# Products with low parts last in each dot and sum, and an earlier split of U on ScalarE

## The reference

```python
def one(tb):                                        # a block of tokens
    ...                                             # scores, two top-k: experts e, gates g
    a = jax.nn.gelu(jnp.einsum('td,thkd->thk', tb, u_tab[e]), approximate=False)
    return jnp.einsum('thk,thkd->td', (g * a).astype(tb.dtype), v_tab[e])
```

## Time and profile before

| | us |
|---|---|
| median of 3 runs (4121.81 to 4129.34) | 4121.95 |
| the profiled execution, its own time | 4132.75 |
| its span from first to last instruction | 4130.9 |
| experts, from the first dot (2104.42) to the last add | about 1941 |
| TensorE busy in the span | 3358.8 (81%) |
| VectorE busy in the span | 2775.2 (67%) |
| GpSimd busy in the span | 1710.3 (41%) |
| ScalarE busy in the span | 1352.9 (33%) |

### The profile page before, as it was taken

One profiled execution on the slowest core, in us unless ns is written; L12 is line 12 of the kernel. 1 busy time (PEld: TensorE's weight loads), 2 busy tenths in 40 slices (PEclk: granted clock), 3 DMA queues, 4 the chain that ended last, 5 costly groups with the idle time before them and its releaser, 6 DMA issues. The chain is left out here.

```text
span 4130.9 us, 59356 instructions
## 1 busy us (share of the span) xinstructions
PE 3358.8 (81%) x20729; PEld 2933.1 (71%) x20729; DVE 2775.2 (67%) x5874; ACT 1352.9 (33%) x3186; POOL 1710.3 (41%) x1341
## 2 busy tenths in 40 slices
PE   6799678565776886466669999999999999999995
PEld 3577455211466786355569999999999999999994
DVE  3114586200024059999968999889899989998885
ACT  3000366100022111578723333333333333333331
POOL 1001000000030432678855556556655655655550
PEclk8899899778678998667779999999999999999997
DMA  6766544799522332254578898889888888988984
GB/s 232 256 223 221 166 151 134 304 408 415 213 87 74 96 107 81 62 117 111 123 257 314 315 332 324 310 315 327 316 309 324 320 320 319 328 318 302 330 286 154
DMA packets 389553, 1001.91 MB, mean 243 GB/s; under 512 B 187044, under 2 KB 232975, under 8 KB 325688
## 3 DMA queue, kind: packets, MB, share of 16 engines
q1 hardware_dynamic: 323768, 491.18, 35.0%
q0 software_dynamic: 62656, 469.86, 31.5%
q10 hardware_dynamic: 2944, 38.77, 2.6%
HBM read 914.75 MB, written 152.04 MB: 258 GB/s over the span
## 5 line engine op out<-in xcount | busy, mean ns | idle before, releaser
L2163 DVE CUSTOM_DVE_ANT_0 e_uv<-e_uv,e_h 128x1024 f32<-128x1024 f32 x416 | 717.2, 1724 | 86.4 <-DMA e_uv<-peer_uv,k_g_idx 85.2
L2232 POOL DMA_INDIRECT e_uv<-peer_uv,k_g_idx x416 | 520.2, 1251 | 547.4 <-DVE e_pY L2175 503.1
L1470 PE MATMUL e_po<-e_ph,e_vh 128*128 128x320 f32 x2048 | 646.8, 316 | 55.9 <-DVE k_OT L2207 49.5
L1470 PE MATMUL e_pa<-k_hi_d,e_uh 128*128 128x320 f32 x2048 | 640.4, 313 | 59.7 <-POOL e_ul L2223 43.3
L1472 PE MATMUL e_pa<-k_hi_d,e_ul 128*128 128x320 f32 x2048 | 634.4, 310 | 0.0
L1471 PE MATMUL e_pa<-k_lo_d,e_uh 128*128 128x320 f32 x2048 | 634.3, 310 | 0.0
L1472 PE MATMUL e_po<-e_ph,e_vl 128*128 128x320 f32 x2048 | 634.0, 310 | 0.0
L1471 PE MATMUL e_po<-e_pl,e_vh 128*128 128x320 f32 x2048 | 634.0, 310 | 0.0
L2175 DVE SCALAR_TENSOR_TENSOR e_pY<-e_uv,e_wts,e_pY 128x1024 f32<-128x1024 f32 x412 | 525.8, 1276 | 0.0
L1470 PEld LDWEIGHTS e_po<-e_ph,e_vh 128*128 128x128 f32 x2048 | 385.5, 188 | 79.0 <-DVE k_OT L2207 64.9
L1470 PEld LDWEIGHTS e_pa<-k_hi_d,e_uh 128*128 128x128 f32 x2048 | 385.9, 188 | 73.0 <-issue 51.8
(11 more groups left out here) (301 smaller groups left out, 5974.9 us busy)
## 6 DMA issues: line engine op xcount, KB each, us to landing
s_kv<-kv_pages SPq DMA_DIRECT2D x128, 512.0 KB, 6.8
s_kv<-kv_state SPq DMA_DIRECT2D x32, 2048.0 KB, 17.3
e_v<-peer_uv SPq DMA_DIRECT2D x128, 512.0 KB, 6.4
e_u<-peer_ut SPq DMA_DIRECT2D x126, 512.0 KB, 6.1
s_g<-r_G SPq DMA_DIRECT2D x10, 4096.0 KB, 21.1
k_OT<-s_g SPq DMA_DIRECT2D x128, 320.0 KB, 5.7
k_win_sample<-state_k_win ACTq DMA_DIRECT2D x28, 1168.0 KB
v_win_sample<-state_v_win POOLq DMA_DIRECT2D x28, 1168.0 KB, 9.8
```

Source lines behind the costliest of these rows:

```text
L1470: nc.tensor.matmul(out, lhs_hi, rhs_hi, start=start, stop=False)
L2163: nc.vector.tensor_tensor_reduce(uv[:, r, 0:D], uv[:, r, 0:D], h[:], 1.0, 0.0, ALU.mult, ALU.add, dots[:, r:r + 1]).then_inc(row_dotted, 1)
L2232: nc.gpsimd.indirect_dma_start(uv[:, s % RING], None, io["peer_uv"], bass.IndirectOffsetOnAxis(ap=keep.g_idx[:, s:s + 1], axis=0),).then_i ...
```

## The change

In `dot`, TensorE waits for the high part of U alone, makes the 16 products with it (high x high and high x low for 8 k), then in the first block waits for the low part, and makes the 8 products with it. In `out`, each sum is now four products vh x ph, four vl x ph and four vh x pl; ahead of them it waits for `vh_done` and `ph_done`, ahead of the second four (n = 0 only) for `vl_done`, ahead of the third four (k = 0 only) for `pl_done`. On ScalarE, U's splits of m = 1 and m = 3 go from behind e_ph to ahead of the wait for `p_done`, between the gelu and e_ph.

```diff
 def dot(i, c):
-    pe.wait_ge(ul_done, CQ * i + c + 1)
+    pe.wait_ge(uh_done, CQ * i + c + 1)
     for b in range(NBD):
         m = NBD * c + b
         pe.wait_ge(p_done, DOTS * i + m + 1)
         cols = slice(b * WD, (b + 1) * WD)
         for k in range(KC):
-            x = split_product(nc, pa[:, m % 2, 0:WD], uh[:, c % 2, k], ul[:, c % 2, k],
-                              keep.hi_d[:, k, cols], keep.lo_d[:, k, cols], k == 0, k == KC - 1)
+            nc.tensor.matmul(pa[:, m % 2, 0:WD], uh[:, c % 2, k], keep.hi_d[:, k, cols], start=(k == 0), stop=False)
+            nc.tensor.matmul(pa[:, m % 2, 0:WD], uh[:, c % 2, k], keep.lo_d[:, k, cols], start=False, stop=False)
+
+        if b == 0:
+            pe.wait_ge(ul_done, CQ * i + c + 1)
+        for k in range(KC):
+            x = nc.tensor.matmul(pa[:, m % 2, 0:WD], ul[:, c % 2, k], keep.hi_d[:, k, cols], start=False,
+                                 stop=(k == KC - 1))
         x.then_inc(dotted, 1)

 def out(i):
-    pe.wait_ge(vl_done, CQ * i + CQ)
+    pe.wait_ge(vh_done, CQ * i + CQ)
     for b in range(NBD):
         cols = slice(b * WD, (b + 1) * WD)
-        pe.wait_ge(pl_done, DOTS * i + NBD * (CQ - 2) + b + 1)
+        pe.wait_ge(ph_done, DOTS * i + NBD * (CQ - 2) + b + 1)
         for k in range(KC):
             n = KC * b + k
+            rows = slice(k * P, (k + 1) * P)
             pe.wait_ge(added, OUTS * i + n + 1)
             for c in range(CQ):
                 if k == 0 and c == CQ - 1:
-                    pe.wait_ge(pl_done, DOTS * i + NBD * (CQ - 1) + b + 1)
-                x = split_product(nc, po[:, n % SUMS, 0:WD], vh[:, c, k * P:(k + 1) * P],
-                                  vl[:, c, k * P:(k + 1) * P], ph[:, c, cols], pl[:, c, cols],
-                                  c == 0, c == CQ - 1)
+                    pe.wait_ge(ph_done, DOTS * i + NBD * (CQ - 1) + b + 1)
+                nc.tensor.matmul(po[:, n % SUMS, 0:WD], vh[:, c, rows], ph[:, c, cols], start=(c == 0), stop=False)
+
+            if n == 0:
+                pe.wait_ge(vl_done, CQ * i + CQ)
+            for c in range(CQ):
+                nc.tensor.matmul(po[:, n % SUMS, 0:WD], vl[:, c, rows], ph[:, c, cols], start=False, stop=False)
+            if k == 0:
+                pe.wait_ge(pl_done, DOTS * i + NBD * (CQ - 1) + b + 1)
+            for c in range(CQ):
+                x = nc.tensor.matmul(po[:, n % SUMS, 0:WD], vh[:, c, rows], pl[:, c, cols], start=False,
+                                     stop=(c == CQ - 1))
             x.then_inc(summed, 1)
...
 def gelus(i, m):
     ...
     nc.scalar.activation(pa[:, m % 2, 0:WD], pa[:, m % 2, 0:WD], ACT.Gelu).then_inc(gelu_done, 1)
+    if b == 1 and c < 2:
+        split_u(CQ * i + 2 + c)
     act.wait_ge(p_done, n + 3)
...
         gelus(i, m)
-        if m % NBD == 1 and m // NBD < 2:
-            split_u(CQ * i + 2 + m // NBD)
         if m in V_AT:
```

## The result

The changed kernel takes 4168.4 us in the median of 4 runs (4163.97 to 4176.4), the kernel before 4123.51 us (4 runs): the ratio is 1.0108, 95% interval 1.0087 to 1.013. It is slower, by 45 us (36 to 54). Its profiled execution took 4164.41 us, 31.7 us more than that of before (4132.75), its span is 4162.6 us. Measured again later beside other kernels, the pair gave 1.0093 (1.0067 to 1.012).

The account below looks back on a forecast made before the run. The bound was taken to be the circle VectorE, ScalarE, VectorE, with GpSimd entering through VectorE. Parts 0, 0 and 30 x 1.1 = +33 us gave 4166 us profiled, 4155 us median; own range 4140 to 4170, 8-in-10 range 4118 to 4172.

Parts of the forecast that it names:

- Part 1: TensorE's new order and waits: the stall before m=4 goes, but ScalarE hardly waits for TensorE; 0, bounds -22.7 and 0.
- Rival (a): TensorE's stalls were the bound, so removing 22.7 us of them gives 4099 us; chance 6%.
- Part 2: U's split at m=1 moved up on ScalarE: GpSimd is held by its own queue, e_ul starts no earlier; 0.
- Part 3: U's split at m=3 moved up: e_ul asks for the ports 1.06 us earlier, ahead of e_pl; +1.1 us a round.
- the replay: The round shown, recomputed from e_ul of m=3 to e_act of m=6: sum 2.20 us late, +1.1 us at the end.
- the collision: At m=3, e_ul comes in while the row dot runs and goes ahead of e_pl; next sum starts 2.20 us late.
- Rival (b): At m=3 VectorE's queue keeps the ports and e_pl goes first, or the meeting is missed; 4122 us, chance 15%.
- the precedent of the earlier trace: First round of the kernel before: e_ul, arriving inside a row dot, went ahead of e_pl, which took 2.67 us.
- Rival (c): The collision at m=3 happens but nothing comes back: 2.20 x 31 = +68 us, 4190 us; chance 7%.
- The price of a round: Delay of e_act of m=6 per round, +1.1 us, range 0.6 to 1.6, counted for 30 rounds.
- the sentence that nothing in the sums gives time back: After e_act of m=6, VectorE is full in the sums and TensorE waits for it, so the +1.1 us stays.

Follow-up runs that it names:

- the held one: Changed kernel plus a GpSimd wait for e_pl of m=3 before it subtracts U's chunk there, against the kernel before: 4121.44 us, 1.0016.
- the kernel with all subtractions placed: TensorE's new order, ScalarE's U splits as before, U's and V's subtractions on GpSimd moved by waits and order, against the kernel before: 4037.05 us, 0.9799.
- the kernel with the early load: Changed kernel with SyncE issuing U's load for m=3 ahead of V's, about 2 us earlier, against the kernel before: 4169.75 us, 1.0137.

## Why the prediction was right, point by point

The sign, the half of the change that does it, and the place were right, and the time lies in the range and in the narrower one (4140 to 4170); 4155 was 13 us short. For the profiled execution the sum gave 4166 us, and it took 4164.41. The 13 us lie in the step from there to the median: the profiled execution of before was 10.8 us above its median, which the prediction took off, and the one of the changed kernel was 4.0 us below its own. So how close 4155 came owes something to luck.

*Part 1, TensorE's order, 0:* shown by that half alone (1.0006). Standing for 0 was the row that the gelu waits 8.4 us for TensorE. The stall went, and a new one before dot m=6, forecast at 1.7 us, came: 1.72 us in the median round. Rival (a) fell with this. The prediction counts three new waits a sum; they are three in all 16 sums of a round, which changes nothing in its sum.

*Part 2, the split at m=1, 0:* shown by the kernel with it alone (1.0003).

*Part 3, the split at m=3:* the replay held step by step. In us behind the start of e_vl of m=2, forecast and traced in the round shown above: e_ul 3.64 and 3.81, sum 6.83 and 6.85, e_act of m=4 8.02 and 8.05, its row dot 8.42 and 8.45, e_act of m=6 13.27 and 13.20. Holding e_ul behind e_pl gave nearly all of it back, so the collision is shown to be the cause, not only argued.

*Rival (b)*, that e_pl would keep the ports, didn't occur in a single round: the precedent of the earlier trace rows held. *Rival (c)*, nothing given back: the row dot behind e_act of m=4 was free in the round shown, and 0.76 us came back.

*The price of a round*, 1.1 us, can be checked in two ways. Over rounds 1 to 31 the way from e_vl of m=2 to e_act of m=6 is 13.43 us in the mean in the changed kernel. In the kernel before it is 12.35 us, 1.08 less (34 us in all; by the medians 13.19 against 12.11), as forecast. But that mean holds two rounds in which ScalarE waited for a transfer (25, for U 0.8 us; 30, for V 3.8 us) and the way was 15.0 and 15.5 us. In the three kernels without the collision (TensorE's half alone, m=1 alone, the held one) it is 12.17 to 12.19: 1.25 us a round, 39 us. Two things that the sum didn't have are in the changed kernel:

- U's load was given its median, 6.1 us. The text looked at a late one, and put an early one under rival (b), as a way to miss the collision. That step is wrong: an early one makes it worse. When the split is over before the row dot starts, the row dot is held to 4.03 us, and e_act of m=6 is at 13.80 instead of 13.19 (+0.6 us).
- The clock was not in the sum. In rounds 3, 4 and 17 the stall before dot m=6 was 2.3 us, the dot ran at the lower clock, its gelu was late, and e_act of m=6 at 15.06 to 15.09 (+1.3 us more); in rounds 1 and 5, with the same stall, it did not. In the second trace of the changed kernel one of six such rounds had it.

Together these are 7 us of this trace. The other way round, the sentence that nothing in the sums gives time back is not quite right: whole rounds (1 to 30, from e_act of m=0 to the next) are 61.26 us in the mean against 60.41 before, 0.85 us longer, so some 0.2 us of the 1.1 came back. That these pieces make up the difference between +33 and +45 in the unprofiled runs isn't shown: the profiled pair differs by 31.7 us only, and the second comparison gave 35 to 38.

## What to carry to other kernels

When an engine is made to start sooner, ask what will be running on the engines that share something with it at that moment; here an idle GpSimd was harmless, and an early one stopped the engine that sets the time. Placing such work by waits and a changed order, so that it runs beside instructions that don't compete, took 2% off (0.9799), while removing a visible stall of an engine that nobody waits for took nothing. A wait that moves work off one competing instruction has to be checked for the next one in line.

## What the runs showed of the hardware

- A subtraction on GpSimd (128x1024, 2.4 us) and a two-input instruction of VectorE from SBUF exclude each other for the whole of their time: in the round shown e_ul ends at 3059.94 and e_pl, free 0.48 us long, comes out at 3060.29. When both queue behind a running row dot, GpSimd's went first in 26 rounds of the changed kernel and in the precedent, though VectorE's was next on its own engine. That they exclude each other is what the Trainium skill's page "SBUF — State Buffer", section "SBUF: two separate sides", says. The same page, section "Who interferes with whom", says that issue order decides who blocks; the traces agree, as e_ul was free to go 0.3 us or more before e_pl in those rounds.
- Two subtractions back to back leave no room between them: e_pl of m=2 takes 3.4 us, and e_pl of m=5 3.37 us in the kernel with all subtractions placed.
- Not expected: a row dot that starts while the gather runs is done in 1.21 us when e_uh is finished only after its start, and in 4.03 us when e_uh was finished before it, although e_ul starts at the same 3.6 us in both cases. In the changed kernel, behind e_vl of m=2: e_uh over at 2.80 to 2.99 us with the row dot held, at 2.98 and from 3.09 on not (the row dot starts at 3.09). So the one that starts first in the trace isn't always the one that runs first, other than the rule has it that the prediction takes from the Trainium skill. That e_uh was finished early isn't enough by itself either: in round 1 of the same trace an e_pl starts at 2191.85, during a gather and 0.9 us ahead of an e_ul whose e_uh was over at 2189.64, and takes its 0.48 us. Why, the traces don't show.
- TensorE's clock, 1.00 in nearly the whole stage, fell to the lower level (1.2 GHz) about the start of dot m=6 in 19 of the 29 rounds in which it had stood 2.3 us ahead of it (the kernel with the early load), and in none of the 31 in which it had stood 1.9 us (the same with the old order). The changed kernel's two traces have it in 3 of 5 and in 1 of 6 rounds with 2.3 us. The length of the stall alone doesn't tell it: ahead of dot m=2 TensorE had stood 1.9 us in round 4 of the kernel with the early load and in round 20 of the held one, and the dot then took 5.3 us, at the lower clock.
